# Seven block products in place of eight for six of eleven feed-forward units

## What is computed

```python
def swiglu_ffn(x, w_in, w_out):
    gate, up = jnp.split(x @ w_in, 2, axis=-1)
    return (jax.nn.silu(gate) * up) @ w_out
# x = x + 0.5 * swiglu_ffn(rms_norm(x, g), w_in, w_out);  w_in 1024 x 5632, w_out 2816 x 1024
```

## Time and profile before

| what | value |
|---|---|
| median of three runs | 887.65 us (887.44 to 887.65) |
| span of the profiled execution, first to last instruction | 886.7 us |
| TensorE busy | 879.4 us |
| VectorE, ScalarE, GpSimd busy | 564.5, 421.7, 78.3 us |
| one inner feed-forward stage | 181.3 us |

### The profile page before, as it was taken

How to read it: one execution, slowest core, us unless ns; L and a number is a source line. 1 busy time by engine, 2 the same in 40 slices (tenths; PEclk the granted TensorE clock), 3 DMA queues, 4 the chain that set the end, 5 groups by cost and what they waited for, 6 DMA issues and landing times.

```text
span 886.7 us, 11328 instructions
## 1 busy us (share of the span) xinstructions
PE 879.4 (99%) x4102; PEld 735.1 (83%) x4102; DVE 564.5 (64%) x598; ACT 421.7 (48%) x471; POOL 78.3 (9%) x70
## 2 busy tenths in 40 slices
PE   9999999999999999999999999999999999999997
PEld 8888888889888888888888888888899888888886
DVE  5875565658966766556577556555687666655643
ACT  7644453538845634345345444343663445434432
POOL 1000000428820000000020000000300000000000
PEclk9999999999999999999999999999999999999999
DMA  8987567555254875776728756746575368675722
GB/s 284 289 260 244 195 199 252 165 178 192 71 189 138 290 237 184 243 241 216 240 84 296 255 187 212 240 168 210 187 286 169 117 196 270 223 235 164 243 67 83
DMA packets 152812, 181.74 MB, mean 205 GB/s; under 512 B 8205, under 2 KB 137257, under 8 KB 152776
## 3 DMA queue, kind: packets, MB, share of 16 engines
q1 hardware_dynamic: 152184, 180.72, 62.3%
q10 hardware_dynamic: 592, 0.53, 0.2%
HBM read 168.11 MB, written 1.05 MB: 191 GB/s over the span
## 4 chain that ended last, share of the span: by engine, by line
PE 99%; DVE 0%; ACT 0%; POOL 0%; issue 0%; POOLq 0%; DVEq 0%
PE acc L1322 11%; PE acc L1324 11%; PE acc L1323 11%; PE ga L1322 11%; PE ga L1324 10%; PE ub L1324 10%; PE ga L1323 10%; PE ub L1323 10%; PE ub L1322 10%; PE tp L1396 1%; PE ga L1592 1%; PE ga L1509 1%; PE tp L1679 0%; PE ub L1626 0%; PE tp L1605 0%; PE tp L1616 0%
## 5 line engine op out<-in xcount | busy, mean ns | idle before, releaser
L915 DVE TENSOR_TENSOR w_lo<-raw,w_hi 128x2048 fp32r<-128x2048 f32 x143 | 324.6, 2293 | 67.7 <-ACT w_hi L604 67.6
L604 ACT ACTIVATE w_hi<-raw 128x2048 fp32r<-128x2048 f32 x151 | 284.6, 1908 | 20.5 <-DMA raw<-in_ffn_w_in_dram 17.2
L1322 PE MATMUL acc<-w_hi,act_hi 128*128 128x512 f32 x416 | 163.1, 392 | 0.0
L1324 PE MATMUL acc<-w_hi,act_lo 128*128 128x512 f32 x416 | 161.8, 389 | 0.0
L1323 PE MATMUL acc<-w_lo,act_hi 128*128 128x512 f32 x416 | 161.7, 389 | 0.0
L1322 PE MATMUL ga<-w_hi,xn_hi 128*128 128x512 f32 x384 | 150.8, 393 | 0.1
L1324 PE MATMUL ga<-w_hi,xn_lo 128*128 128x512 f32 x384 | 149.5, 389 | 0.0
L1322 PE MATMUL ub<-w_hi,xn_hi 128*128 128x512 f32 x384 | 149.5, 389 | 0.0
L1323 PE MATMUL ga<-w_lo,xn_hi 128*128 128x512 f32 x384 | 149.5, 389 | 0.0
L1323 PE MATMUL ub<-w_lo,xn_hi 128*128 128x512 f32 x384 | 149.5, 389 | 0.0
L1324 PE MATMUL ub<-w_hi,xn_lo 128*128 128x512 f32 x384 | 149.5, 389 | 0.0
(11 more groups left out here) (173 smaller groups left out, 677.3 us busy)
## 6 DMA issues: line engine op xcount, KB each, us to landing
raw<-in_ffn_w_in_dram SPq DMA_DIRECT2D x172, 512.0 KB, 5.1
raw<-in_ffn_w_out_dram SPq DMA_DIRECT2D x88, 512.0 KB, 4.0
xs<-xs SPq DMA_DIRECT2D x176, 64.0 KB, 2.1
raw<-in_sgu_w_in_dram SPq DMA_DIRECT2D x16, 512.0 KB, 4.8
raw<-in_ab_w_in_dram SPq DMA_DIRECT2D x12, 512.0 KB, 5.0
raw<-in_ab_w_out_dram SPq DMA_DIRECT2D x8, 512.0 KB, 3.7
raw<-in_sgu_w_out_dram SPq DMA_DIRECT2D x8, 512.0 KB, 4.2
raw<-in_ffn_w_in_dram SPq DMA_DIRECT2D x8, 256.0 KB, 5.5
```

The source lines that it names most:

```text
L604: act.activation(w_hi[:, n % RING, :], raw[:, n % RAW, :], ACT.Copy).then_inc(hi_split, 1)
L915: dve.tensor_tensor(w_lo[:, n % RING, :], raw[:, n % RAW, :], w_hi[:, n % RING, :].bitcast(F32), ALU.subtract).then_inc(lo_split, 1)
L1322: pe.matmul(dst, s_hi, m_hi, start=start, stop=False)
L1324: return pe.matmul(dst, s_lo, m_hi, start=False, stop=stop)
```

## The change

Units 3 to 10 except 5 and 8 are taken in three pairs, (3, 4), (6, 7) and (9, 10). For a pair the token matrix is four blocks (t by half), the weights are four blocks (half by unit), and the 2 x 2 block product is made with seven products instead of eight, in the form with shared sums. `multiply` is one block product: 4 chunks x 3 passes = 12 matmuls, so a pair takes 84 in place of 96. The stage has 42 slabs: the seven of each pair are at places B11, B21, T1, T2, B22, T3, T4 of the tables below, where B are blocks of the weights and T are sums of them.

- VectorE makes the sums T1 = B11 + B12 and T2 = T1 + B22 (`sum_one`, `sum_two`), GpSimd makes T3 = B12 + B22 and T4 = T2 + B21 (`sum_three`, `sum_four`), all 128 x 2048, in two places in `scratch` (`chain`, `other_chain`). Each of the seven slabs then gets a high part from ScalarE and a low part.
- GpSimd makes the low parts of six slabs of each stage (`POOL_LOW`); the other 36 are VectorE's.
- The four sums of token blocks are made once a stage (`side_one` to `side_four`, 128 x 512, with a high and a low part each) and live in place 5 of the ring, which leaves five places for slabs until the last T3 is used. A fourth raw buffer is in `scratch`.
- The products of a pair run in banks `tp`. Three copies by ScalarE (`keep_first`, `keep_in_gates`) and three adds by VectorE (`join`, 128 x 512, one input in PSUM) put the partial results together. The transposes of the norm go to the `acc` banks instead.
- The turn of the hidden rows has two pairs of buffers, in `xs` and in `gain`. The loops are written out, with an order of its own for the first stage. The DMAs, fills and transposes that the mixers need move from the ffn stages to their ends or into the mixers.

The core of the diff (the lists of VectorE and ScalarE are long; the stretch around the second pair stands for them):

```diff
--- before.py
+++ after.py
@@ -21,12 +21,8 @@
...
-def at(count, per, i):
-    return count if i is None else i * per + count
...
+    UA, UB, B11, B21, T1, T2, B22, T3, T4 = ((4, 16, 28), (5, 21, 36), (6, 17, 29), (7, 18, 30), (9, 20, 32),
+                                             (11, 22, 33), (12, 24, 34), (13, 25, 35), (15, 27, 37))
+    UNITS = (0, 1, 2, 4, 3, 5, 7, 6, 10, 8, 9)
+    OUT_AT = (8, 10, 14, 19, 23, 26, 31, 38, 39, 40, 41)
+    SECOND, FIRST = (3, 6, 8), (4, 7, 10)
+    PAIRS_IN = len(B11)
+    POOL_LOW = (10, 14, 21, 26, 31, 36)
+    FFN_SLABS, MIX0_SLABS, MIX1_SLABS = 42, 10, 12
+    SUMS_END = T4[-1] + 1
...
-        order += [("norm", k, t, h) for t in range(TT) for h in ((0, 1) if k else (1,))]
+        for i in range(slabs_of[kind]):
+            n = base[k] + i
+            if kind == "ffn" and i == 2:
+                sums_free[k] = freed[RING - 1]
+            if kind == "ffn" and i == SUMS_END:
+                freed[RING - 1] = base[k] + T3[-1] + 1
+            places = RING - 1 if kind == "ffn" and 2 <= i < SUMS_END else RING
+            slot = min(range(places), key=lambda c: freed[c])
+            slot_of.append(slot)
+            free_after.append(freed[slot])
+            freed[slot] = n + 1
...
+        def turn_homes(k, v):
+            if (ffn0[k] + v) % 2:
+                return gain[:, k % 2, 0:WIDE], gain[:, k % 2, WIDE:]
+            return xs[:, 0, 0:WIDE], xs[:, 1, 0:WIDE]
...
+            def load_chain(j, w, half, unit):
+                src = in_view(w)[:, 4 * half:4 * half + 4]
+                for to, c in zip(columns((chain, other_chain)[j]), pair(unit * WIDTH, FF)):
+                    sp.dma_start(to, src[:, :, c]).then_inc(chain_landed[j], 16)
...
+                        to_turn(k, 2)
+                        rows_of(UA[1], 0, 5)
+                        out_of(3, 19)
+                        rows_of(B21[1], 1, 6)
+                        sp.wait_ge(lo_split, b + T3[0] + 1)
+                        load_chain(1, w_in, 0, 7)
+                        rows_of(UB[1], 1, 5)
+                        sp.wait_ge(lo_split, b + T4[0] + 1)
+                        load_chain(0, w_in, 0, 6)
+                        out_of(4, 23)
+                        to_turn(k, 3)
+                        rows_of(B22[1], 1, 7)
+                        to_turn(k, 4)
+                        out_of(5, 26)
+                        rows_of(B21[2], 1, 9)
...
+            def sum_three(k, g):
+                p, n = PAIRS_IN * (ffn0[k] // STEPS) + g, base[k] + B22[g]
+                pool.wait_ge(first_sum, p + 1)
+                pool.wait_ge(raw_landed[raw_of[n][0]], 32 * raw_of[n][2])
+                pool.tensor_tensor(other_chain, other_chain, slab(n), ALU.add).then_inc(third_sum, 1)
+            def sum_four(k, g):
+                p, n = PAIRS_IN * (ffn0[k] // STEPS) + g, base[k] + B21[g]
+                pool.wait_ge(lo_split, base[k] + T2[g] + 1)
+                pool.tensor_tensor(chain, chain, slab(n), ALU.add).then_inc(fourth_sum, 1)
+            def low(n):
+                pool.wait_ge(hi_split, n + 1)
+                pool.tensor_tensor(w_lo[:, slot_of[n], :], slab(n), w_hi[:, slot_of[n], :].bitcast(F32),
...
+                    b = base[k]
+                    sum_three(k, 0)
+                    low(b + 10)
+                    sum_four(k, 0)
+                    low(b + 14)
+                    low(b + 21)
+                    sum_three(k, 1)
+                    sum_four(k, 1)
+                    low(b + 26)
+                    low(b + 31)
+                    sum_three(k, 2)
+                    sum_four(k, 2)
+                    low(b + 36)
...
+            def split(n):
...
+                    act.wait_ge(raw_landed[raw_of[n][0]], 32 * raw_of[n][2])
+                if free_after[n]:
+                    act.wait_ge(slab_used, free_after[n])
...
+            def side_hi_of(k, j):
+                if j == 0:
+                    act.wait_ge(slab_used, sums_free[k])
+                act.wait_ge(side_sum, 4 * (ffn0[k] // STEPS) + j + 1)
+                act.activation(sums_hi[:, j, :, :], side[j % 2].rearrange("p (a t) -> p a t", a=4), ACT.Copy)\
+                    .then_inc(side_hi, 1)
+            def keep_first(k, g):
+                act.wait_ge(side_ready, 4 * (ffn0[k] // STEPS) + 4)
+                if g:
+                    act.wait_ge(ga_free, fill0[k] + FIRST[g - 1] + 1)
+                act.wait_ge(slab_used, base[k] + B11[g] + 1)
+                act.activation(side[0], bank_x[:, :], ACT.Copy).then_inc(kept, 1)
+            def keep_in_gates(k, g, t, what, bank):
+                act.wait_ge(blocks_ready, TT * (ffn0[k] + SECOND[g]))
+                act.wait_ge(slab_used, base[k] + what + 1)
+                act.activation(sgh[:, :, t, :], bank[:, :].rearrange("p (a n) -> p a n", a=2), ACT.Copy)\
+                    .then_inc(kept, 1)
...
+            def side_lo(k, j):
+                dve.wait_ge(side_hi, 4 * (ffn0[k] // STEPS) + j + 1)
+                dve.tensor_tensor(sums_lo[:, j, :, :], side_of(j % 2), sums_hi[:, j, :, :].bitcast(F32),
+                                  ALU.subtract).then_inc(side_ready, 1)
...
+            def side_two(k):
+                dve.wait_ge(side_sum, 4 * (ffn0[k] // STEPS) + 1)
+                if k:
+                    side_less(1, 0, normed(0, 0), True)
...
+            def sum_one(k, g):
+                dve.wait_ge(chain_landed[1], 32 * (pair_of(k, g) + 1))
+                dve.tensor_tensor(chain, chain, other_chain, ALU.add).then_inc(first_sum, 1)
+            def sum_two(k, g):
+                n = base[k] + B22[g]
+                dve.wait_ge(raw_landed[raw_of[n][0]], 32 * raw_of[n][2])
+                dve.tensor_tensor(chain, chain, slab(n), ALU.add).then_inc(second_sum, 1)
+            def join(k, g, j):
+                at, copies, to, bank = ((B21, 1, side[0], bank_z[:, :]),
+                                        (B22, 3, sgh[:, :, 0, :], bank_z[:, :].rearrange("p (a n) -> p a n", a=2)),
+                                        (T3, 3, sgh[:, :, 1, :], bank_x[:, :].rearrange("p (a n) -> p a n", a=2)))[j]
+                dve.wait_ge(kept, 3 * pair_of(k, g) + copies)
+                dve.wait_ge(slab_used, base[k] + at[g] + 1)
+                dve.tensor_tensor(to, bank, to, ALU.add).then_inc(joined, 1)
...
+                        product_rows(1, g + 10, late)
+                        to_blocks(1, f + 5, k)
+                        split_to(b + 28)
+                        hidden_lo(k, 5)
+                        join(k, 1, 1)
+                        second_product(k, 1, 0)
+                        second_blocks(k, 1, 0)
+                        join(k, 1, 2)
+                        second_product(k, 1, 1)
+                        second_blocks(k, 1, 1)
+                        first(k, 1, 0)
+                        first_blocks(k, 1, 0)
+                        split_to(b + 31)
+                        first(k, 1, 1)
+                        sum_one(k, 2)
+                        hidden_lo(k, 6)
...
+            def multiply(n, bank, tok_hi, tok_lo, start):
+                slab_ready(n)
+                for a in range(4):
+                    o = slice(a * WIDE, (a + 1) * WIDE)
+                    mm = three(bank[:, :], tok_hi[:, a, :], tok_lo[:, a, :], w_hi[:, slot_of[n], o],
+                               w_lo[:, slot_of[n], o], start and a == 0, a == 3, not start)
+                mm.then_inc(slab_used, 1)
...
+            def first_product(k, g):
+                if g == 0:
+                    pe.wait_ge(small_free, before_stage[k])
+                else:
+                    pe.wait_ge(ub_free, fill0[k] + FIRST[g - 1] + 1)
+                multiply(base[k] + B11[g], bank_x, xn_hi[:, 0:4, 0:P], xn_lo[:, 0:4, 0:P], True)
...
+                multiply(base[k] + B21[g], bank_z, xn_hi[:, 4:8, 0:P], xn_lo[:, 4:8, 0:P], True)
+            def fifth_product(k, g):
+                pe.wait_ge(joined, 3 * (PAIRS_IN * (ffn0[k] // STEPS) + g) + 1)
+                pe.wait_ge(side_ready, 4 * (ffn0[k] // STEPS) + 4)
+                multiply(base[k] + T1[g], bank_z, sums_hi[:, 0], sums_lo[:, 0], True)
+            def sixth_product(k, g):
+                pe.wait_ge(kept, 3 * (PAIRS_IN * (ffn0[k] // STEPS) + g) + 1)
...
+            def fourth_product(k, g):
+                pe.wait_ge(joined, 3 * (PAIRS_IN * (ffn0[k] // STEPS) + g) + 3)
+                multiply(base[k] + T4[g], bank_x, xn_hi[:, 4:8, P:2 * P], xn_lo[:, 4:8, P:2 * P], False)
...
                     unit(b + 2, f + 1)
-                    step(0, True)
...
-                    unit(n, f + STEPS - 1)
+                    unit(b + UA[0], f + 2)
+                    first_product(k, 0)
+                    second_product(k, 0)
+                    pe.wait_ge(side_sum, 4 * (e // STEPS) + 4)
+                    step_out(0)
+                    fifth_product(k, 0)
+                    step_out(1)
+                    sixth_product(k, 0)
```

(72 more changed lines are left out.)

1003 lines of the change are left out of this document (749 added, 254 removed).

## The result

The changed kernel takes 1025.97 us (four runs, 1022.04 to 1029.33) against 887.65 (887.44 to 887.68): 1.155 times as long, 95% interval 1.1525 to 1.1583. Slower was the likelier sign, at 0.56, but 919 was far too little, and the range ended at 945. The 32.6 us of matmuls did go, which alone would have left 855; the time is 171 us above that.

What follows compares the result with a forecast made beforehand. It took TensorE's matmuls to bound the kernel before; afterwards, VectorE's and GpSimd's mutually exclusive work makes a stage 189.4 us, 7.9 over 181.5. Four stages add 31.6 to 886.7, 918.3, and with 0.95 around it 919.3 us; range 855 to 945.

Steps and rivals of the forecast that it cites:

- What bounds the kernel before, and what is removed: Feed-forward stages: only TensorE's matmuls set the time; 144 fewer at 0.2267 us save 32.6 us, 8.2 a stage.
- The exclusion: VectorE instructions with two SBUF inputs and GpSimd's exclude each other; those with a PSUM input or one input run on.
- TensorE stays the bound: Rival, faster: both engines' own sums fit, 143 and 56 of 173 us; 855 to 862 us in all; chance 0.24.
- GpSimd falls into gaps: Rival, faster: GpSimd's instructions lie under VectorE's waits, turns and joins; 862 to 886 us; chance 0.16.
- VectorE's work, 143 us a stage without GpSimd's: Feed-forward stage: 30 us of added low parts, sums and joins on 112.7 make 143 of 173 us.
- the sum of a stage: 37.4 us first part plus three windows, VectorE's and GpSimd's work nearly end to end, 152.0 us: stage 189.4, four stages +31.6.
- Waits in line: Rival, slower still: VectorE's in-order list adds some 4 us a window; 211 us a stage, 1005 in all; chance 0.12.
- TensorE's clock: Clause in the slower rival: the granted clock, 1.00 throughout before, could also fall in the gaps; no size given.
- about 847 us: Sign of being right: TensorE's busy time falls to about 847 us, with 15 to 20 us idle a stage.
- The edits I cost at nothing: Moved mask and share windows in mix0 cost 0 to 2 us, mix1's broadcasts 0 to 3; turning buffers and SyncE waits hidden.
- The ring: Chain of a pair's sums, high and low parts and a load: 31 us against 43.5 of a pair, covered by 12.

Runs made afterwards that it cites:

- e3: Changed kernel with GpSimd's twelve instructions a stage cut to one column each, the rest of those sums and low parts left out: 880.54 us.
- e1: Kernel before, with test instructions behind its end: eight VectorE low parts beside three of GpSimd take 30.59 us; its total means nothing.
- e2: Changed kernel with all low parts and sums on VectorE, order unchanged: 942.31 us.
- e7: Changed kernel with one pair a stage instead of three, all on VectorE, the mixers' small loads, masks and transposes back where they were: 968.86 us.
- e9: The one-pair kernel of e7, all on VectorE, with the order changed at three places: 919.13 us.
- e11: Kernel of e2 with the first pair's join put earlier and the next stage's three first loads ahead of the last turn: 957.83 us.
- e5: Changed kernel with GpSimd's six low parts a stage given back to VectorE, its six sums kept on GpSimd: 983.95 us.
- e6: Changed kernel with GpSimd's six sums a stage moved to VectorE, its six low parts kept on GpSimd: 979.38 us.
- e4: As e3, but 19 small GpSimd memsets ahead of each one-column instruction, so that its results are as late as the full ones: 920.01 us.
- e15: Kernel of e2 with the first pair's join put right after the second sums, and nothing else: 941.32 us.

## Why the prediction was wrong

**What bounds the kernel before, and what is removed:** right. 144 matmuls went, and in e3, where GpSimd holds little, stages take 175.3 to 177.4 us.

**The exclusion:** right, and shown by e1 for whole instructions. The rival that TensorE stays the bound, 0.24, fell with it. So did the one that GpSimd falls into gaps: it needed VectorE's waits and PSUM work to lie under GpSimd's instructions, and VectorE's low parts took 2.64 and 3.00 us.

**VectorE's work, 143 us a stage without GpSimd's:** right. e3 has it at 136 to 144. With what GpSimd holds up VectorE is busy 178 to 189 us, close to the 189.4 of my sum, which laid its list and GpSimd's end to end.

**The step that failed** is the sum of a stage, "Laid end to end that is 53.3, 53.3 and 51.7", up to "Stage: 189.4". It took VectorE as a full pipe, without a wait in it. But it takes its list in order, and stood idle 26 to 34 us of each stage of the changed kernel, for high parts above all (80.8 us in the whole kernel), on top of the work. The stages took 215.0, 214.5, 212.7 and 208.9. I had this as the rival "Waits in line", 211 a stage, and gave it 0.12 because I could name only about 4 us a window. I had read all waits of the earlier trace rows as slack. Those for gates were: 40.1 us in that stage before, 1.1 in the same stage of the changed kernel. Those for high parts were not: 16.6 before, 23.6 after, 21.8 in e2. e2 is the plainest test, since none of GpSimd's sums is in it: 165 us of VectorE's work fit into 173, and the stage takes 195.

**What I left out of the sum:** TensorE's clock, named in one clause of that rival. Of the 171 us above the bound, 38 are matmuls at clock 0.50. They lie in the same time as VectorE's waits, and no run tells how much a full clock would give back. TensorE's busy time rose to 903 us, where I had named about 847 as a sign of being right.

**The edits I cost at nothing:** mix0 takes 79.5 us and mix1 74.5, 6.2 and 2.4 more than before between the same transposes (73.3 and 72.1), against 0 to 2 and 0 to 3. In e7, with the mixer's pieces back in the stage before, mix0 is 75.3; in e9, with two of its slabs split ahead of the last hidden values, as before the change, it is 73.3 and mix1 72.1, the old times. So about 4 us are the moved pieces, and 2.0 and 2.3 the norm; that this stands on VectorE behind the next stage's low part, and that behind its load, is argued and was not tested alone. The loads alone, moved back, did nothing for it (e11: 79.0 and 74.4).

**The ring** as a bound: e5 and e6 speak against it. By e4 the lateness of GpSimd's results still costs 39 us.

**What stays open:** whether another order of three pairs would fit. e15 moved one wait and found it again further on; that is one try. Open too is whether a list with PSUM work beside GpSimd's instructions, as in the last phase of e1, would make GpSimd's help cheap. How much of e2's 59 us of standing is order and how much is room wasn't separated, and one pair's way from 969 to 902 shows that an order can hide much.

## What to carry to other kernels

Where an engine takes its list in order, its idle time ahead of waits is only in part room: here the waits for gates were and those for high parts were not. Cost added work by the lists of who stands behind whom, and take a stage at work plus the waits that remain. Moving an elementwise instruction with two SBUF inputs from VectorE to GpSimd takes 2.2 us off VectorE and can block its next instruction of that kind for 4.5; it cost 1.5 to 1.7 us each here. What blocks is decided by what stands next in the list. And in these kernels a us that TensorE stood cost 1.4 to 1.5 us.

## What the runs showed of the hardware

After many waits TensorE's granted clock was 0.50 for a while: 13 matmuls were slow after 3.59 us (e9), 12 after 5.60 (e2). After e9's waits of 1.0 us none of the next 20 was, nor after any of e3's 18 waits, the longest of which is 1.71 us. The length of the wait doesn't decide alone: in the changed kernel 8 matmuls were slow after a wait of 3.62 us that ended at 682.65, and none after one of 3.63 us that ended at 469.55.

GpSimd suffers too. Its sums at L750 took 6.24 us on average in the changed kernel, 4.56 at the least; in e3 one on a single column took 1.0 to 2.0 us on average, part of which may be waiting for VectorE's instruction to end.

GpSimd's memsets, which read nothing, did not slow VectorE's low parts (2.28 and 2.29 on average in e4; in e1 six took 13.30 us beside memsets, as six alone did).
